# The value products of the preceding step moved in between the turnings of a step's two heads (second block's small attention)

## The chip, the cores and the metric

The kernel runs on one core of a Trainium2 chip. Such a core has TensorE (matrix products, called PE in the rows, its weight loads PEld), VectorE (DVE), ScalarE (ACT), GpSimd (POOL) and SyncE (SP), which work side by side and meet at semaphores. The metric is the time on the device for one execution of the whole program, in microseconds.

## The reference, cut to what matters

Two blocks of two layers each work on 512 tokens of width 1024. In each layer of the second block a mixer stands between two feed-forward networks. One of its parts is an attention with 8 heads of 64 in 2 key groups, in three branches. Two of the branches are computed here as plain causal attentions over all 512 tokens: with 8 blocks of 64 tokens the selection of 8 takes all of them, and the window is 512.

```python
s_s = jnp.einsum('bqgrd,bgqkd->bgrqk', qb, k_sel)
p_s = masked_softmax(s_s, (kpos <= t[:, None])[:, :, None])
o_s = jnp.einsum('bgrqk,bgqkd->bqgrd', p_s.astype(v_sel.dtype), v_sel)
...
s_w = jnp.einsum('bqgrd,bkgd->bgrqk', qb, k_win)
p_w = masked_softmax(s_w, mask_w)
o_w = jnp.einsum('bgrqk,bkgd->bqgrd', p_w.astype(v_win.dtype), v_win)
o = gb[..., 0:1] * o_c + gb[..., 1:2] * o_s + gb[..., 2:3] * o_w
```

## The kernel before, in words

The two branches are one object, `PairedAttention`, with 24 steps in a layer (`steps` = 2 branches x 12). A step handles two heads at once (b = 0 and 1) and one or two query tiles of 128 tokens. Steps come in threes: the first has the tile with four key blocks, the second the tile with three, the third the tiles with two and one. So `blocks(s)` is 4, 3, 3.

What each engine does for a step s:

- `score` (L536), TensorE: queries times keys into a PSUM bank, two steps ahead. It waits until the maxima of the steps up to s - 2 are taken.
- `maximum` (L612), VectorE: mask, scale and row maximum of the scores of both heads.
- `exponentials` (L582), ScalarE: the exponentials of both heads with their row sums.
- `turn` (L546), TensorE: transposes the probabilities of one head, block by block, into the PSUM bank of that head. It waits for that head's exponentials and for the copy of the same head in the step before.
- the copies: VectorE copies head 0 (L621), ScalarE head 1 (L592, behind the exponentials of the next step). The copy of step s - 1 on ScalarE comes after the exponentials of step s.
- `weigh` (L559), TensorE: the value products of a step. They wait for both copies, and in each third step (s % 3 == 0) for the output bank to be taken.
- `take_output` (L2579), ScalarE: copies the finished output of three steps out of its bank. In the second branch it waits for VectorE's addition of the first branch (L2702).

Around the steps `after(s)` places other work. On TensorE: a product of the pooling part (L2447) in steps 3 and 6, and the spread coefficients (`spread_coefficients`, L2434) in steps 15 to 18. On VectorE: the finishing of the gated linear attention in steps 0 to 7 (L2712 to L2714), and the scaling and adding of the first branch (L2698, L2702) in steps 15 to 18. Behind step 23 TensorE spreads the coefficients of the second branch and begins the output projection (L333, L341).

The order on each engine is the order in which the code is written; the engines take their instructions in that order. Between the small attention of a layer and its surroundings the big weights flow through their own ring: SyncE loads them, ScalarE or VectorE rounds, GpSimd subtracts.

Of the kernel before, what the change touches and what calls it, by code (L numbers as in the profile page):

```python
# [144 lines left out]
def build(nc, dr, out):  # L145
    ctx = ExitStack()
    with ctx:
# [112 lines left out]
        class Project:  # L260
# [115 lines left out]
            def after(self, j, act):  # L376

                u = self.jobs[j][0] if j >= 0 else -1
                if j + 1 == len(self.jobs) or self.jobs[j + 1][0] != u:
                    self.stream.round(act, act.copy, RAW, WP, u + 1 + SLOTS)  # L380
# [3 lines left out]
        class Attention:  # L384
# [56 lines left out]
            def tensor(self, pe):  # L441
                for s in range(self.steps):
                    if s + 2 < self.steps:
                        self.score(pe, s + 2)
                    self.turn(pe, s)
                    if s >= 1:
                        self.weigh(pe, s - 1)
                self.weigh(pe, self.steps - 1)
# [47 lines left out]
        class PairedAttention:  # L496
# [67 lines left out]
            def tensor(self, pe, after):  # L564
                for s in range(self.steps):
                    self.turn(pe, s, 0)
                    self.turn(pe, s, 1)
                    if s + 2 < self.steps:
                        self.score(pe, s + 2)
                    if s >= 1:  # L570
                        self.weigh(pe, s - 1)
                    after(s)
                self.weigh(pe, self.steps - 1)

# [2580 lines left out]
```

## Time and profile before

| what | us |
|---|---|
| median of 3 runs | 3177.47 (3176.85 to 3179.08) |
| profiled execution, its own time | 3176.42 |
| span of the profiled execution | 3174.6 |
| TensorE busy | 3070.6 (97%) |
| VectorE busy | 1241.9 (39%) |
| ScalarE busy | 928.7 (29%) |
| GpSimd busy | 1391.7 (44%) |

The span is the time from the first to the last instruction in the trace; the execution's own time is a little longer. The small attention of the first layer lies at about 1616 to 1697 us, that of the second at 2654 to 2735. The shares of the engines over the whole span tell little about them, since the program is mostly large products. In the rows a time at the start is microseconds from the start of the span; the number behind it is a duration. The bracket at the end is the idle time of the engine just before, and what released it; "issue" is time in which it waited for nothing that the profile shows.

### The profile page before, as it was taken

How to read it: one execution, taken by the hardware profiler on the slowest of the kernel's cores; microseconds unless marked ns; L12 is line 12 of the kernel's file. 1: busy time of each engine (PE TensorE's matmuls, PEld its weight loads, DVE VectorE, ACT ScalarE, POOL GpSimd, SP SyncE). 2: the span in 40 equal slices, each digit the busy share in tenths (PEclk: the TensorE clock that was granted, in tenths of full speed). 3: DMA queues.
4: the chain of work that ended last, by engine and by line, in shares of the span. 5: the costliest groups of instructions: out<-in, count | busy, mean ns of one | idle time of the engine just before them, and what ended most of it. 6: DMA issues, size and time to landing. Idle time of an engine off the chain costs nothing. (4 is left out here: it accounts for less than half of the span.)

```text
span 3174.6 us, 39298 instructions
## 1 busy us (share of the span) xinstructions
PE 3070.6 (97%) x15352; PEld 2478.9 (78%) x15352; DVE 1241.9 (39%) x1997; ACT 928.7 (29%) x1623; POOL 1391.7 (44%) x1074
## 2 busy tenths in 40 slices
PE   8999999989999999999999999999999999999998
PEld 5887777778777788887767888878888776788886
DVE  8466244746433222222375322332222237532233
ACT  4356442435453211103463211021110346421101
POOL 2443445524343545445341544454444434154542
PEclk8999999999999999999999999999999999999999
DMA  6222315213231222232110222222222221022222
GB/s 262 100 82 105 101 57 210 103 67 113 87 110 40 73 101 92 85 97 95 67 41 28 93 97 93 91 90 101 98 85 92 86 80 41 28 92 93 88 91 72
DMA packets 45861, 287.78 MB, mean 91 GB/s; under 512 B 5496, under 2 KB 6008, under 8 KB 18680
## 3 DMA queue, kind: packets, MB, share of 16 engines
q1 hardware_dynamic: 42480, 270.32, 24.2%
q10 hardware_dynamic: 3240, 15.53, 1.5%
q8 instruction: 95, 1.56, 0.2%
q14 instruction: 46, 0.38, 0.0%
HBM read 283.67 MB, written 2.16 MB: 90 GB/s over the span
## 5 line engine op out<-in xcount | busy, mean ns | idle before, releaser
L1926 POOL TENSOR_TENSOR w_parts<-w_raw,w_parts 128x512 fp32r<-128x512 f32 (+1 forms) x544 | 703.2, 1321 | 752.9 <-DVE w_parts L2061 702.4
L1986 PE MATMUL PS<-x_parts,w_parts 128*128 128x512 f32 x4224 | 961.1, 390 | 4.5 <-ACT x_parts L799 4.5
L1986 PEld LDWEIGHTS PS<-x_parts,w_parts 128*128 128x128 f32 x4224 | 793.4, 188 | 173.7 <-issue 5.3
L139 POOL TENSOR_TENSOR w_parts<-w_raw,w_parts 128x512 fp32r<-128x512 f32 x380 | 532.6, 1432 | 820.4 <-ACT w_parts L128 790.6
L369 PE MATMUL PS<-x_parts,w_parts 128*128 128x512 f32 x2784 | 698.6, 397 | 14.8 <-POOL w_parts L139 13.7
L369 PEld LDWEIGHTS PS<-x_parts,w_parts 128*128 128x128 f32 x2784 | 521.2, 189 | 135.5 <-POOL w_parts L139 17.8
L2027 PE MATMUL PS<-hidden_parts,w_parts 128*128 128x512 f32 x2112 | 482.9, 390 | 0.0
L2027 PEld LDWEIGHTS PS<-hidden_parts,w_parts 128*128 128x128 f32 x2112 | 396.2, 188 | 83.8 <-issue 1.9
L2068 DVE TENSOR_TENSOR ffn_buffers<-PS,ffn_buffers 128x512 f32<-128x512 f32 x88 | 60.9, 692 | 732.1 <-PE PS L1986 708.9
L128 ACT CAST w_parts<-w_raw 128x2048 fp32r<-128x2048 f32 (+1 forms) x92 | 172.1, 1870 | 140.6 <-PE PS L369 52.3
L2061 DVE CAST w_parts<-w_raw 128x2048 fp32r<-128x2048 f32 (+1 forms) x144 | 156.9, 1089 | 113.4 <-PE PS L2027 113.4
L2045 ACT CAST hidden_parts<-ffn_buffers 128x512 f32 (+1 forms) x88 | 55.0, 625 | 483.8 <-DVE ffn_buffers L2068 483.8
L313 PE MATMUL PS<-w_parts,x_parts 128*128 128x512 f32 x768 | 185.4, 399 | 1.4 <-ACT ssd_buffers L1389 1.4
L313 PEld LDWEIGHTS PS<-w_parts,x_parts 128*128 128x128 f32 x768 | 143.8, 188 | 38.4 <-issue 7.2
L2043 ACT ACTIVATE ffn_buffers<-PS 128x512 f32<-128x512 f32 x88 | 52.7, 599 | 338.3 <-PE PS L1986 338.3
L2087 DVE SCALAR_TENSOR_TENSOR x_all<-PS,x_all 128x512 f32<-128x512 f32 x32 | 22.1, 692 | 225.6 <-PE PS L2027 225.6
L1769 ACT ACTIVATE ffn_buffers<-x_all 128x512 f32<-128x512 f32 x28 | 17.6, 633 | 290.5 <-DVE x_all L2087 231.7
L372 PE MATMUL PS<-w_parts,x_parts 128*128 128x256 f32 x768 | 96.6, 285 | 3.0 <-POOL w_parts L139 3.0
L372 PEld LDWEIGHTS PS<-w_parts,x_parts 128*128 128x128 f32 x768 | 93.3, 192 | 6.7 <-POOL w_parts L139 3.9
L582 ACT ACTIVATE mixer_buffers<-mixer_buffers 128x512 f32<-128x512 f32 (+3 forms) x128 | 70.6, 553 | 25.9 <-DVE mixer_buffers L612 25.9
L369 PE MATMUL PS<-mixed_low,w_parts 128*128 128x512 f32 x192 | 75.9, 396 | 0.0
L333 PE MATMUL PS<-x_parts,w_parts 128*128 128x512 f32 x192 | 54.8, 415 | 10.0 <-ACT x_parts L1874 8.6
(396 smaller groups left out, 3116.2 us busy)
## 6 DMA issues: line engine op xcount, KB each, us to landing
w_raw<-in_w_gu SPq DMA_DIRECT2D x88, 1024.0 KB, 4.7
w_raw<-in_w_in SPq DMA_DIRECT2D x70, 1024.0 KB, 4.8
w_raw<-in_w_d SPq DMA_DIRECT2D x64, 704.0 KB, 4.0
w_raw<-in_w_out SPq DMA_DIRECT2D x24, 1024.0 KB, 4.8
m_all<-in_w_next SPq DMA_DIRECT2D x14, 1024.0 KB, 8.2
m_all<-in_w_gate SPq DMA_DIRECT2D x8, 1024.0 KB, 4.8
ssd_buffers<-decay_rows ACTq DMA_DIRECT2D x16, 512.0 KB, 3.9
m_all<-in_w_next ACTq DMA_DIRECT2D x2, 1024.0 KB, 14.1
```

What stands on the lines that cost most here:

```text
L128: op(parts[:, self.slot(u), 0, 0:n], raw[:, self.slot(u), 0:n]).then_inc(self.high, 1)
L139: last = pool.tensor_tensor(parts[:, self.slot(u), 1, at:to], raw[:, self.slot(u), at:to], parts[:, self.slot(u), 0, at:to].bitcast(F32), ...
L313: last = pe.matmul(PS[:, self.bank(j), 0:m], XS[:, a, kt * second + k, c * P:(c + 1) * P], w[b][:, k, :], start=(not second and k == 0 and ...
L369: last = pe.matmul(PS[0:m, self.bank(j), :], w[a][:, k, c:c + m], part(b, k), start=start, stop=stop)
L372: last = pe.matmul(PS[:, j % 2, 0:m], part(a, k)[:, c * P:(c + 1) * P], w[b][:, k, :], start=start, stop=stop)
L582: act.activation(self.p[:, s % 2, b, at:at + n], self.p[:, s % 2, b, at:at + n], ACT.Exp, bias=self.nm[:, 2 * tile + b:2 * tile + b + 1], ...
L1926: last = pool.tensor_tensor(WP[:, b, 1, at:to], RAW[:, b, at:to], WP[:, b, 0, at:to].bitcast(F32), ALU.subtract)
L1986: return pe.matmul(PS[:, 2 * b + g, :], WP[:, slot(b), w, c:c + P], XS[:, x, k, :], start=start, stop=stop)
L2027: last = pe.matmul(PS[:, 4 + m % 2, :], WP[:, slot(b), w, k * P:(k + 1) * P], hid[:, x, b * KH + k, :], start=(b == k == n == 0), stop=(b ...
L2045: act.copy(flat(hid[:, 0, bass.ds(u, 1), :]), pt[:, b, :]).then_inc(self.hid_high, 1)
L2061: dve.tensor_copy(WP[:, slot(b), 0, 0:n], RAW[:, slot(b), 0:n]).then_inc(self.high, 1)
L2068: dve.tensor_tensor(pt[:, b, :], PS[:, 2 * b + 1, :], gs[:, b, :], ALU.mult).then_inc(self.product, 1)
```

## The change

In `PairedAttention.tensor` the value products of step s - 1 stand between the turning of head 0 and the turning of head 1 of step s. The scores of step s + 2 stand behind both, as before, and are now the last of the step.

```diff
             def tensor(self, pe, after):
                 for s in range(self.steps):
                     self.turn(pe, s, 0)
+                    if s >= 1:
+                        self.weigh(pe, s - 1)
                     self.turn(pe, s, 1)
                     if s + 2 < self.steps:
                         self.score(pe, s + 2)
-                    if s >= 1:
-                        self.weigh(pe, s - 1)
                     after(s)
                 self.weigh(pe, self.steps - 1)
```

The rows below are TensorE's program; `x6` counts instructions as written. L546 are turnings, L536 scores, L559 value products. First two steps of the second branch of the second layer (steps 12 and 13), before the change:

```order
L546 MATMUL PS<-cst,mixer_buffers 128x128 x8
L536 MATMUL PS<-mixer_buffers 128x256 x2
L536 MATMUL PS<-mixer_buffers 128x128 x2
L559 MATMUL PS<-mixer_buffers 64x128 x6
L546 MATMUL PS<-cst,mixer_buffers 128x128 x6
L536 MATMUL PS<-mixer_buffers 128x512 x2
L559 MATMUL PS<-mixer_buffers 64x128 x8
```

The same two steps on TensorE after it:

```order
L546 MATMUL PS<-cst,mixer_buffers 128x128 x4
L559 MATMUL PS<-mixer_buffers 64x128 x6
L546 MATMUL PS<-cst,mixer_buffers 128x128 x4
L536 MATMUL PS<-mixer_buffers 128x256 x2
L536 MATMUL PS<-mixer_buffers 128x128 x2
L546 MATMUL PS<-cst,mixer_buffers 128x128 x3
L559 MATMUL PS<-mixer_buffers 64x128 x8
L546 MATMUL PS<-cst,mixer_buffers 128x128 x3
L536 MATMUL PS<-mixer_buffers 128x512 x2
```

Each run of turnings is cut in two by the value products, and the scores now touch the turnings of the next step.

The second place is steps 15 to 17 on TensorE, where L2434, the spread coefficients, end each step. It begins with those of step 15. Before:

```order
L2434 MATMUL PS<-cst,mixer_buffers 64x128 x8
L546 MATMUL PS<-cst,mixer_buffers 128x128 x6
L536 MATMUL PS<-mixer_buffers 128x512 x2
L559 MATMUL PS<-mixer_buffers 64x128 x8
L2434 MATMUL PS<-cst,mixer_buffers 64x128 x8
```

After:

```order
L2434 MATMUL PS<-cst,mixer_buffers 64x128 x8
L546 MATMUL PS<-cst,mixer_buffers 128x128 x3
L559 MATMUL PS<-mixer_buffers 64x128 x8
L546 MATMUL PS<-cst,mixer_buffers 128x128 x3
L536 MATMUL PS<-mixer_buffers 128x512 x2
L2434 MATMUL PS<-cst,mixer_buffers 64x128 x8
```

The value products of step 15, which wait for an output tile to be taken, had all turnings and the scores of step 16 ahead of them and now have one head's turnings.

The third place is the end of the attention on TensorE, steps 22 and 23 and the coefficients of the second branch. Before:

```order
L546 MATMUL PS<-cst,mixer_buffers 128x128 x6
L559 MATMUL PS<-mixer_buffers 64x128 x8
L546 MATMUL PS<-cst,mixer_buffers 128x128 x6
L559 MATMUL PS<-mixer_buffers 64x128 x12
L2434 MATMUL PS<-cst,mixer_buffers 64x128 x32
```

After:

```order
L546 MATMUL PS<-cst,mixer_buffers 128x128 x3
L559 MATMUL PS<-mixer_buffers 64x128 x8
L546 MATMUL PS<-cst,mixer_buffers 128x128 x6
L559 MATMUL PS<-mixer_buffers 64x128 x6
L546 MATMUL PS<-cst,mixer_buffers 128x128 x3
L559 MATMUL PS<-mixer_buffers 64x128 x6
L2434 MATMUL PS<-cst,mixer_buffers 64x128 x32
```

The last two sets of value products stood together behind the last turning; now the last turning stands between them.

The other engines' instructions and their order are the same.

## Rows read from the trace of the kernel before

**Rows 1.** Timeline, first layer, TensorE: value products of step 15 (start, duration, ...).

```profile
1670.55 1.09 PE L559 MATMUL PS<-mixer_buffers 128*64 128x128 f32 x16 [0.42 <-ACT mixer_buffers L2579]
```

**Rows 2.** Chain of waits, second layer, steps 9 to 12 (start, duration, what).

```profile
2686.57 1.02 PE PS L546 x8
...
2688.44 0.81 PE PS L559 x12
...
2690.05 1.06 PE PS L536 x4
...
2692.94 0.84 PE PS L536 x4
...
2694.59 1.02 PE PS L546 x8
```

**Rows 3.** Windows: TensorE, its loads, VectorE, ScalarE, GpSimd busy; clock, DMA share, GB/s.

```profile
2670.00:2676.00 6.00, 6.00 (x54) 4.11 (x52) 5.86 (x17) 4.51 (x12) 0.00 (x0) 1.00 0.00 0
```

**Rows 4.** Chain of waits, second layer, steps 15 to 18.

```profile
2705.30 0.90 PE PS L2434 x16
...
2707.73 0.59 ACT mixer_buffers L2579
...
2708.46 1.09 PE PS L559 x16
2709.55 0.89 PE PS L2434 x16
...
2714.55 0.63 PE PS L546 x4
```

**Rows 5.** Timeline, second layer: TensorE's weight loads and two of its products.

```profile
2646.23 1.77 PE L536 MATMUL PS<-mixer_buffers 64*128 64x512 f32 x8 [0.69 <-ACT mixed L2489]
2647.93 0.44 PE L2375 MATMUL PS<-cst,mixer_buffers 128*128 128x128 f32 x2
...
2689.18 0.64 PEld L546 LDWEIGHTS PS<-cst,mixer_buffers 128*128 128x128 f32 x6 [0.17 <-issue]
2689.98 0.30 PEld L536 LDWEIGHTS PS<-mixer_buffers 64*128 64x128 f32 x4 [0.17 <-issue]
...
2712.60 0.91 PEld L2434 LDWEIGHTS PS<-cst,mixer_buffers 128*64 128x64 f32 x16
...
2730.12 1.36 PEld L559 LDWEIGHTS PS<-mixer_buffers 128*64 128x64 f32 x24 [0.17 <-issue]
```

**Rows 6.** Timeline, second layer, around a maximum and around a tile's copy.

```profile
2663.06 0.55 DVE L612 CUSTOM_DVE_ANT_0 mixer_buffers<-PS,cst 128x384 f32<-128x384 f32 x1
...
2665.33 0.58 ACT L2579 COPY mixer_buffers<-PS 128x512 f32<-128x512 f32 x1
...
2688.37 0.88 PE L559 MATMUL PS<-mixer_buffers 128*64 128x128 f32 x12
2688.49 0.42 DVE L612 CUSTOM_DVE_ANT_0 mixer_buffers<-PS,cst 128x256 f32<-128x256 f32 x1 [0.61 <-PE PS L536]
```

**Rows 7.** Timeline, second layer, the last steps.

```profile
2729.07 0.46 ACT L592 COPY mixer_buffers<-PS 128x384 f32<-128x384 f32 x1
...
2729.67 0.52 PE L546 MATMUL PS<-cst,mixer_buffers 128*128 128x128 f32 x3 [0.55 <-ACT mixer_buffers L592]
...
2730.22 0.48 ACT L592 COPY mixer_buffers<-PS 128x384 f32<-128x384 f32 x1 [0.70 <-PE PS L546]
...
2731.52 3.69 PE L2434 MATMUL PS<-cst,mixer_buffers 128*64 128x128 f32 x64
```

**Rows 8.** What line 2579 waited for, second layer (us, times).

```profile
  PE PS L559: 4.3, 4
```

**Rows 9.** Timeline and chain around step 8, and the window with its clock.

```profile
2681.57 0.55 PE L546 MATMUL PS<-cst,mixer_buffers 128*128 128x128 f32 x3 [3.24 <-ACT mixer_buffers L582]
...
2683.77 1.58 PE PS L536 x4
...
2684.00:2686.00 2.00, 2.00 (x12) 0.92 (x12) 0.60 (x3) 0.54 (x3) 0.00 (x0) 0.50 0.00 0
```

## The prediction

> Names: in step s of the small attention the TensorE program holds T0 and T1 (the turnings of the two heads, L546), S (the scores of step s+2, L536) and W (the value products of step s-1, L559); in four steps also F (the spread coefficients, L2434). Times are of the second layer; the first layer repeats the pattern to 0.01 us at the places read [rows 1].
>
> **What bounds the kernel now.** I read the chain of waits over the attention first, then the timeline of TensorE's weight loads, then VectorE and ScalarE around single steps. In the second half of each attention the chain never leaves TensorE from step 9 to step 15: three steps take 2694.59 - 2686.57 = 8.02 us, and the pieces fill them without a hole [rows 2]. So there a step costs what TensorE's instructions cost. Steps 1 to 7 are VectorE's: 5.86 of 6 us busy [rows 3], because it also finishes the gated attention's tiles there. From step 15 to 23 the chain hops: F, VectorE's scaling, ScalarE's taking of an output tile (L2579), W, F, and so on [rows 4]. Behind the attention TensorE runs into the output projection without a hole, so what is late at the last F (2731.52) is late at the end. The profiled execution took 3176.42 us (span 3174.6); the median shown is 3177.47, 1.05 above.
>
> **What a change of kind costs.** T uses the array as 128\*128, S as 64\*128, W and F as 128\*64. Between kinds the weight loads show 0.17 us of idle put down to nothing but issue: W to T at 2689.18, T to S at 2689.98, and, at the end of the attention, T to W at 2730.12. Where the kind stays (W to F, 2712.60) no idle is shown [rows 5]. Six turnings take 0.64 us, so three take 0.32. S leaves no such sign in the loads, but S with 512 columns takes 1.06 and with 384 takes 0.84 [rows 2]: the four quarters of difference are 0.22, so 512 columns would be 0.87 and about 0.2 is fixed. From S to a turning the same shows: eight score instructions and the change take 1.70 (2646.23 to 2647.93) [rows 5], 1.49 of it columns at the same rate. The Trainium skill says as much in "TensorEngine Tiling (Array Packing)", Key Properties: changing the tiling mode drains the engine. By that rule the trace agrees, and it speaks against this change.
>
> **The change, part by part.** Nothing is computed anew; W moves from behind S to between T0 and T1. Orders on the other engines and the DMA queue are untouched. Before, a step has three changes of kind (T-S, S-W, W-T), now four (T0-W, W-T1, T1-S, S-T0). In steps with F: before three (W-F costs none), now five.
>
> (a) TensorE-bound steps, 9 to 15: six steps x 0.17 = 1.02, and step 15, with F, 0.17 + 0.2 = 0.37. Together 1.39. Step 8 adds nothing: its extra change lies in the wait for ScalarE's copy, which W inherits from T1.
>
> Does W now wait in these steps? It needs the copy of head 1 that T1 needed at the same place, so no wait is added by that. But S now comes just ahead of the next step, so the loop S, maximum, exponentials, copy, W has lost W's cover. The tightest is the one with an output tile in it: 0.12 from the end of S to VectorE (2688.37 to 2688.49), 2.27 from the maximum to the tile's copy (2663.06 to 2665.33) [rows 6], and 0.73 from there to W [rows 4] = 3.12. TensorE has in that time one whole step, a third of 8.02 and one change, 2.84, and T0 of three turnings with its change, 0.49: 3.33. It fits by 0.2, so 0 is added; if it missed, VectorE and ScalarE would set the pace at a few tenths a step.
>
> (b) Step 16. Its W needs the tile taken (L2579), and that needs VectorE's addition behind F of step 15 [rows 4]. Before, T1 and S stood ahead of W and were done in this wait, with 0.42 still left. Now they stand behind: from W to the F of step 16 TensorE must do, besides W, the change 0.17, T1 0.32 + 0.17 and S 1.06 = 1.72. That F is on the chain (2709.55, then VectorE's scaling and maximum, ScalarE's exponentials and copy, TensorE again at 2714.55), so 1.72 late. What is queued behind the waiting W is T1, S and F; VectorE waits for all three.
>
> (c) Steps 17 and 18: TensorE reaches W of step 18 about 0.15 behind the copy, and one change more stands ahead of F: 0.3 together. Steps 19 to 22: W and T1 wait for the same copies, order inside does not count; the exponentials of step 23 started behind W and an output tile (1.08 us waited) and now start behind S: + 0.15.
>
> (d) The end. Before, T1 of step 23 started at 2729.67, then W of 22, and under it ScalarE's copy (2730.22); W of 23 followed with no wait, F at 2731.52: 1.85. Now: W of 22 0.64, change 0.17, T1 start to copy 0.55, copy to TensorE 0.60 (2729.07 to 2729.67), W of 23 0.64 = 2.60 [rows 5, 7]. The copy has lost its cover: + 0.75 to 0.8.
>
> (e) Steps 1 to 7: S ends later by W of the step and a change, at most 1.02 + 0.17 (W of four blocks: 16 loads at the rate of 2730.12, and its change). VectorE's own load covers it: it goes into its maximum at 2663.06 with no idle before it [rows 6] and is full in the whole window [rows 3]. Cost 0; with that cover gone it would be 0.17 a step, 1.2 a layer.
>
> Sum per layer 1.39 + 1.72 + 0.3 + 0.15 + 0.8 = 4.36; two layers 8.7. 3176.42 + 8.7 = 3185.1 on the profiled execution's scale, 3186.2 on the median's. I take 3186.
>
> Bounds. T0-W was read once, at a place where both sides were ready; if the four-change order paid nothing for it, (a) would be 0 and (b) to (d) about 2.2 per layer: 3181.9. Below nothing only by the first rival. Above: the clock, the third rival.
>
> **Rivals.**
> Faster: W earlier lets ScalarE take the output tile earlier. It waited for W four times in a layer, 4.3 us [rows 8]. If these waits carry the pace, up to 1.08 at each of those that lie on the chain would come back. Against it: three of the four lie in the TensorE-bound steps, and the fourth is replaced by S's wait. Giving the full 1.08 at the last one in both layers, with free changes and (d) hidden, and (b) halved, it is 2 x (0.86 - 1.08) = -0.4; to be faster by more than 0.2% (6.4 us, about what a measurement of this kernel can tell) all three mid ones must count too: 3177.5 + 2 x 0.86 - 8.6 = 3170.6. It decides from where ScalarE, not TensorE, ends last before W.
>
> No measurable change: the changes of kind are free, (b) and (d) alone remain: 3181.9, + 0.14%. For it: 0.17 is put down to "issue", not to a named cause. Against: it appears at each change of kind in either direction.
>
> More slower: the clock. Before step 8 TensorE idled 3.24 us, and then ran at 0.50 of full speed, the lower of the levels 1.2 and 2.4 GHz; S with 384 columns took 1.58 there [rows 9] against 0.84, and T1, S and W together, 2.14 at full speed, by the same ratio 4.0. In step 16 the idle time ahead of W grows from 0.42 to about 2. If the clock falls there too, up to 1.9 per layer more, of which I take 1.5: 3189. The Trainium skill, "TensorE: Matmul & The Clock Gate", on practice, warns only of idle gaps over some 3 us; by that rule it does not happen. For falling: the time around is full of small matmuls; against: the idle time stays shorter than the one that was followed by a fall.
>
> **Numbers.** Forecast as summed 0.62; clock rival 0.12; free changes 0.21; faster rival 0.05. Of the forecast's cases a tenth or so ends under +0.2% (3183.8) by terms that are smaller than read. So slower 0.68, same 0.28, faster 0.04. The range that holds 8 in 10 reaches to the free-changes case below and to the clock case above: 3181 to 3189.5.
>
> **What would show it.** In the trace after: three steps of 9 to 14 take 8.5 us instead of 8.02, the weight loads with 0.17 of idle on both sides of W; in step 16 W still waits for the tile's copy, now about 2 us, and F starts 2.8 instead of 1.1 us behind W's start; at the end W of 23 waits for ScalarE's copy; VectorE's steps 1 to 7 unmoved; granted clock 1.00 around step 16. It would be wrong if T0 to W shows no idle, if W in steps 10 and 13 waits for ScalarE (more), or if the last F moves less than 4 us against the attention's start.

## The result, and the profile after

| runs | before | after | ratio (95%) |
|---|---|---|---|
| first set | 3178.96 (3176.85 to 3179.73, 7 runs) | 3187.91 (3186.31 to 3191.68, 7 runs) | 1.0033 [1.0023, 1.0043] |
| the same kernel once more | 3177.12 | 3188.69 (3187.55 to 3190.46, 5 runs) | 1.0037 [1.0023, 1.0050] |
| profiled execution | 3176.42 | 3189.43 | |

The change makes the kernel slower, by 0.33% in the first set. The median of before shown ahead of the prediction, 3177.47, was that of its first three runs. The medians of the 7 runs differ by 8.95 us and those of the second set by 11.57 (ratios of 1.0033 and 1.0037, some 10.5 and 11.8 us); the forecast was 8.7. The traces tell more than these medians. I measure an attention from the first turning of step 0 to the first coefficient product behind step 23:

| us | before | after | difference |
|---|---|---|---|
| first layer | 1616.29 to 1693.61 = 77.32 | 1617.48 to 1700.52 = 83.04 | +5.72 |
| second layer | 2654.01 to 2731.52 = 77.51 | 2661.38 to 2744.57 = 83.19 | +5.68 |

So 11.4 of the 13.0 us between the profiled executions lie in the two attentions; 1.2 arose ahead of the first one and 0.4 between and behind them. Per layer that is 1.3 more than the 4.36 of the sum. The page's totals:

```profile
span 3187.6 us, 39298 instructions
...
PE 3078.3 (97%) x15352; PEld 2479.8 (78%) x15352; DVE 1242.0 (39%) x1997; ACT 930.8 (29%) x1623; POOL 1393.0 (44%) x1074
```

VectorE, ScalarE and GpSimd are busy as long as before to 2 us. TensorE shows 7.7 us more, though its work is the same: its instructions are longer somewhere.

**Steps 9 to 14.** The chain of waits of the second layer, from T0 of step 12 to T0 of step 15, answers to [rows 2]:

```profile
2702.46 0.59 PE PS L546 x4
2703.05 0.81 PE PS L559 x12
2703.85 0.59 PE PS L546 x4
2704.44 0.85 PE PS L536 x8
...
2710.94 0.59 PE PS L546 x4
```

Still all TensorE, and a step now has four pieces instead of three. Three steps (12, 13, 14) take 2710.94 - 2702.46 = 8.48, where it was 8.02: 0.46, or 0.153 a step. The weight loads of the second layer, here of step 10, show where, as [rows 5] did:

```profile
2697.22 0.85 PEld L559 LDWEIGHTS PS<-mixer_buffers 128*64 128x64 f32 x16 [0.17 <-issue]
2698.24 0.31 PEld L546 LDWEIGHTS PS<-cst,mixer_buffers 128*128 128x128 f32 x3 [0.17 <-issue]
2698.72 0.30 PEld L536 LDWEIGHTS PS<-mixer_buffers 64*128 64x128 f32 x4 [0.17 <-issue]
```

The idle 0.17 stands on both sides of the value products now. A border between two groups costs little where the kind stays: the six turnings of [rows 5] are those of both heads, each with a wait of its own, and take 0.64 without a hole.

**Step 16**, first layer, TensorE:

```profile
1669.59 1.09 PE L2434 MATMUL PS<-cst,mixer_buffers 128*64 128x128 f32 x16
1670.62 0.55 PE L546 MATMUL PS<-cst,mixer_buffers 128*128 128x128 f32 x3
1672.97 1.47 PE L559 MATMUL PS<-mixer_buffers 128*64 128x128 f32 x16 [1.80 <-ACT mixer_buffers L2579]
1674.37 0.90 PE L546 MATMUL PS<-cst,mixer_buffers 128*128 128x128 f32 x3
1675.20 1.98 PE L536 MATMUL PS<-mixer_buffers 64*128 64x512 f32 x4
1677.11 1.09 PE L2434 MATMUL PS<-cst,mixer_buffers 128*64 128x128 f32 x16
```

The wait of W is 1.80 instead of 0.42 [rows 1], since T1 and S no longer stand in it. From W to F it is 1677.11 - 1672.97 = 4.14; before it was 0.89 (1670.55 to 1671.44; the chain in [rows 4] sets F of this step 0.2 later than the timeline does). But not only are there more instructions: each is longer. T1 takes 0.90, two rows above 0.55. The windows (columns as in [rows 3]) say why:

```profile
1672.00:1674.00 2.00, 1.03 (x15) 1.06 (x16) 1.73 (x10) 1.76 (x6) 0.00 (x0) 0.88 0.00 0
1674.00:1677.00 3.00, 3.00 (x12) 1.04 (x8) 0.00 (x0) 1.06 (x5) 0.00 (x0) 0.51 0.00 0
1677.00:1680.00 3.00, 3.00 (x38) 2.21 (x36) 1.72 (x3) 0.00 (x0) 0.00 (x0) 1.00 0.00 0
```

After the idle 1.80 us the granted clock stood at 0.51 for three microseconds, the lower of its two levels (1.2 and 2.4 GHz). Meanwhile VectorE shows 0.00: it waits for F. The second layer has the same wait of 1.80 and the same fall:

```profile
2719.00:2721.00 2.00, 2.00 (x7) 0.50 (x6) 0.00 (x0) 0.48 (x1) 0.00 (x0) 0.50 0.00 0
```

There W starts at 2717.08 and F at 2720.97, 3.89 later, and F itself takes 1.30 instead of 1.09: the stretch at the lower clock begins a little later and reaches into F.

**The end**, chain of waits of the second layer, against [rows 7]:

```profile
2741.88 0.88 PE PS L559 x12
2742.76 0.49 PE PS L546 x3
2743.25 0.02 issue
2743.28 0.49 ACT mixer_buffers L592
2743.76 0.14 issue
2743.90 0.88 PE PS L559 x12
```

ScalarE's copy is on the chain now: the value products of step 23 wait for it.

**ScalarE's waits.** What line 2579 waited for in the second layer, against [rows 8]:

```profile
  PE PS L559: 1.1, 1
```

Three of four waits, 3.2 us, are gone. Nothing ended earlier by that.

### The profile page after: what moved, and what is told of

It is laid out like the page before. It is cut to its first block and busy times, and to the rows that moved or that the text cites. A ratio compares the mean times of both kernels' runs of the same rounds, so it can differ in the third digit from the quotient of the medians.

```text
span 3187.6 us, 39298 instructions
## 1 busy us (share of the span) xinstructions
PE 3078.3 (97%) x15352; PEld 2479.8 (78%) x15352; DVE 1242.0 (39%) x1997; ACT 930.8 (29%) x1623; POOL 1393.0 (44%) x1074
## 5 line engine op out<-in xcount | busy, mean ns | idle before, releaser
L1986 PE MATMUL PS<-x_parts,w_parts 128*128 128x512 f32 x4224 | 961.7, 390 | 4.5 <-ACT x_parts L799 4.5
L369 PE MATMUL PS<-x_parts,w_parts 128*128 128x512 f32 x2784 | 696.7, 396 | 15.4 <-POOL w_parts L139 14.3
L612 DVE CUSTOM_DVE_ANT_0 mixer_buffers<-PS,cst 128x512 f32<-128x512 f32 (+3 forms) x128 | 56.1, 487 | 27.9 <-PE PS L536 27.7
```

The lines of the kernel that those rows point to most:

```text
L369: last = pe.matmul(PS[0:m, self.bank(j), :], w[a][:, k, c:c + m], part(b, k), start=start, stop=stop)
L612: dve.tensor_tensor_reduce(self.p[:, s % 2, b, at:at + n], PS[:, 2 * (s % 2) + b, at:at + n], const("causal")[:, T - n:T], -(HD ** -0.5), ...
L1986: return pe.matmul(PS[:, 2 * b + g, :], WP[:, slot(b), w, c:c + P], XS[:, x, k, :], start=start, stop=stop)
```

## The experiments

Pieces and attentions are read from the profiled executions; a time given with a ratio, or for the whole program, is the median of the runs. W in step 16 means, as in the prediction, the value products that stand in step 16 of TensorE's program (those of step 15). In the diffs "-" is the kernel before, where nothing else is said. Kernels with added lines have the line numbers behind them shifted by 2 to 5 in their rows.

### Step 16 and the clock

The changed kernel once more:

> The changed kernel unaltered, profiled and timed again. Theory (changes of kind, lost cover in step 16 and at the end, and a fall of the granted clock behind the longer idle time of step 16): each small attention takes 5.7 us more than before from its first turning to the spread coefficients of the second branch (83.0 against 77.3), of which about 1.5 is the clock in step 16 (granted clock about 0.5 there). Rival (the clock fell by chance of that one execution): the three instruction groups behind the wait of step 16 run at full speed in one or both layers, value products to spread coefficients 2.6 instead of 4.1, and the attention takes 4.2 more.

Attentions 82.96 and 83.23. From W to F of step 16 4.14 and 4.03 us, with 1.80 idle ahead: the clock fell again in both layers.

The new order in step 16 alone:

```diff
+                    between = s == 16
                     self.turn(pe, s, 0)
+                    if s >= 1 and between:
+                        self.weigh(pe, s - 1)
                     self.turn(pe, s, 1)
                     if s + 2 < self.steps:
                         self.score(pe, s + 2)
-                    if s >= 1:
+                    if s >= 1 and not between:
                         self.weigh(pe, s - 1)
```

> The order of the change in step 16 alone, all other steps as before. Theory (lost cover of one turning and the scores behind the wait for the output tile, plus the clock): from the value products of step 15 to the spread coefficients behind them 4.1 us instead of 0.9 in each layer, 3.2 more, at a granted clock near 0.5; the whole attention 3.2 to 3.3 more per layer, the program 6.5 more. Rival (the clock does not fall, since fewer changes of kind came before): 1.7 per layer, 3.5 in all. Rival (the cost of the change lies in the changes of kind): under 0.5 per layer. Steps 9 to 15 as before: three steps 8.02.

3180.95 us, ratio 1.0013 [1.0004, 1.0023]; attentions 80.67 and 80.75, so +3.35 and +3.24. First layer:

```profile
1670.61 1.09 PE L559 MATMUL PS<-mixer_buffers 128*64 128x128 f32 x16 [1.80 <-ACT mixer_buffers L2582]
...
1672.11 1.98 PE L536 MATMUL PS<-mixer_buffers 64*128 64x512 f32 x4
1674.02 1.88 PE L2437 MATMUL PS<-cst,mixer_buffers 128*64 128x128 f32 x16
```

Second layer:

```profile
2713.38 1.09 PE L559 MATMUL PS<-mixer_buffers 128*64 128x128 f32 x16 [1.80 <-ACT mixer_buffers L2582]
...
2714.88 1.13 PE L536 MATMUL PS<-mixer_buffers 64*128 64x512 f32 x4
2715.94 1.09 PE L2437 MATMUL PS<-cst,mixer_buffers 128*64 128x128 f32 x16
```

The same wait of 1.80; in the first layer the scores take 1.98 and F 1.88, in the second 1.13 and 1.09. So the fall doesn't always come. (In the first layer it came late: W still takes 1.09, W to F is 3.41 instead of the expected 4.1, and F carries the rest.) Where it stays away, W to F takes 2.56, which is 1.67 over 0.89: term (b), forecast at 1.72. The second layer lost its other 1.5 elsewhere, in its windows around step 8:

```profile
2686.00:2688.00 2.00, 1.68 (x7) 1.01 (x7) 0.13 (x1) 1.96 (x6) 0.80 (x1) 0.50 0.00 0
2688.00:2690.00 2.00, 2.00 (x16) 1.15 (x12) 1.04 (x4) 0.57 (x2) 0.00 (x0) 0.50 0.00 0
2690.00:2692.00 2.00, 2.00 (x12) 1.57 (x8) 0.66 (x1) 0.74 (x4) 0.00 (x0) 0.50 0.00 0
```

There the clock stayed down for over 6 us (the slow stretch, from here on); the kernel before shows some 3.5 us at this place, where it too idles 3.05 and 3.24 us ahead of step 8 [rows 9]. From T0 of step 8 to W in step 16 it is 2713.38 - 2684.98 = 28.40 here and 2708.46 - 2681.57 = 26.89 before, 1.51 less. So this attention's +3.24 matches the expected 3.2 by luck: 1.67 of it is step 16.

The changed kernel with the wait filled by products that nobody reads (the kernel's own `keep_busy`, in a free bank), first three of them:

```diff
                     self.turn(pe, s, 0)
+                    if s == 16:
+                        pe.wait_ge(self.copied[1], s)
+                        keep_busy(pe, 5, 3)
                     if s >= 1:
                         self.weigh(pe, s - 1)
```

(The unmarked lines are those of the changed kernel.)

> The changed kernel with three products of the identity with a constant (128x512, into the PSUM bank that the next turning overwrites) put into TensorE's wait of step 16, behind the first head's turning. They compute nothing that is used and fill about 1.3 of the 1.8 us of idle time. Theory (the clock fell because of that idle time): the granted clock stays at 1.00, value products to spread coefficients 2.6 instead of 4.1, the attention 81.5 instead of 83.0 per layer, the program 3 less than the changed kernel. Rival (the clock falls for the small matmuls around, whatever stands in the wait): 4.1 as in the changed kernel.

The three took 2.67, more than the wait, so W went 0.7 late: this part of the expectation's price was mis-sized. Attentions 82.14 and 83.52; 3189.15 us, ratio 1.0039 [1.0023, 1.0054]. But W to F was 2.56 and 2.57, at a granted clock of 1.00. The second attention has the longer slow stretch at step 8 again. The same with two products (`keep_busy(pe, 5, 2)`):

> The changed kernel with two unused products (128x512, into the bank that the next turning overwrites) in TensorE's wait of step 16; a product of this kind took 0.87 us in the kernel with three, so two take 1.74 of the 1.80 us of idle time and the value products start on time. Theory: the clock stays at 1.00, value products to spread coefficients 2.6, wait not longer than before, and the attention 81.5 against 83.0 in both layers. Rival (the products only move the loss): 82 or more.

```profile
1670.64 1.88 PE L649 MATMUL PS<-cst 128*128 128x512 f32 x4
1672.60 1.09 PE L559 MATMUL PS<-mixer_buffers 128*64 128x128 f32 x16
...
1675.17 1.09 PE L2437 MATMUL PS<-cst,mixer_buffers 128*64 128x128 f32 x16
```

The window of the same layer:

```profile
1672.00:1675.00 3.00, 2.92 (x25) 1.49 (x23) 1.36 (x9) 2.69 (x10) 0.00 (x0) 1.00 0.03 5
```

No idle, clock 1.00, W to F 1675.17 - 1672.60 = 2.57 in place of 4.14: the clock cost 1.57 us. The first attention is 81.44, 1.6 less than in the changed kernel. The second, 83.03, gained only 0.2: from T0 of step 0 to F of step 15 it took longer, 53.7 against 52.1 in the first layer, again by a longer slow stretch at step 8. One run of the whole: 3186.47.

Taken together, 1.80 us of idle time was followed by the lower clock in 5 of 6 attentions (twice two of the changed kernel, one of two here), and no filled wait was, in 4 of 4. The waits ahead of step 8 say the same. In the twelve kernels profiled here that leave it unfilled it is 2.20 to 3.33 us long, and the lower clock followed in all 24 attentions; in the two that fill it (below) it followed in none of 4. That the idle time causes the fall is shown by this; what decides whether it comes behind 1.80 us is not.

### The other terms

The change everywhere but in step 16, and then everywhere but in 16 and 23 (the diff of before with other conditions, `between = s != 16` and `between = s not in (16, 23)`):

> The order of the change in all steps but 16. Theory: the 1.7 and the clock's 1.5 of step 16 are gone, the changes of kind (1.2) and the end (0.8) stay: the attention 2.3 to 2.6 us more than before per layer (79.8), idle time ahead of the value products of step 16 again 0.4, granted clock 1.00 there; the program 5 more than before. Rival (the loss is spread over the steps, the wait of step 16 only moves to the next tile): the attention stays above 82.

> The order of the change in all steps but 16 and 23. Theory: against the order changed in all steps but 16 (2.4 more than before per layer) the lost cover of the last copy goes too, 0.84: the attention 1.5 to 1.7 more than before (79.0), value products of step 22 to spread coefficients 1.85 again, what stays are the changes of kind. Rival (the end is hidden by ScalarE's tile): 79.8 as without it.

Without 16: 3182.34, ratio 1.0016 [1.0006, 1.0025]; attentions 79.75 and 79.98, +2.43 and +2.47. The sum less (b) is 4.36 - 1.72 = 2.64. Step 16 keeps its short wait and full speed:

```profile
1672.38 1.09 PE L559 MATMUL PS<-mixer_buffers 128*64 128x128 f32 x16 [0.41 <-ACT mixer_buffers L2582]
1673.28 1.07 PE L2437 MATMUL PS<-cst,mixer_buffers 128*64 128x128 f32 x16
```

Without 16 and 23: 3179.84, ratio 1.0010 [1.0001, 1.0020]; attentions 78.91 and 80.26. The first is 0.84 less than without 16 alone: term (d), forecast at 0.8. From the wait for the copy to F it is 1.85 again (1693.24 to 1695.09). In the second layer a longer slow stretch at step 8 hides it: T0 of step 0 to F of step 15 took 53.45, against 52.11 in the first.

### Where the scores stand

Scores between the turnings, value products last. That has four changes of kind too, but no wait of W moved up:

```diff
                     self.turn(pe, s, 0)
-                    self.turn(pe, s, 1)
                     if s + 2 < self.steps:
                         self.score(pe, s + 2)
+                    self.turn(pe, s, 1)
                     if s >= 1:
                         self.weigh(pe, s - 1)
```

> The scores of step s+2 between the two turnings, the value products behind both: first head, scores, second head, value products. As many changes of kind in a step as in the changed kernel (four), but the value products keep their cover. Theory (each change of kind costs 0.17 where TensorE sets the pace, whichever work stands between the turnings): three steps of 9 to 14 take 8.5 us as in the changed kernel, not 8.02; no further loss in step 16 and at the end, and the scores now fill waits between the two turnings in steps 8, 18 and 20, up to 1.3 together: the attention 77.2 to 78.2 against 77.3 before. Rival (the cost of those steps comes from the value products standing early, not from changes of kind): three steps 8.02.

3176.39 against 3176.34, ratio 0.9999 [0.9989, 1.0008]; attentions 77.00 and 77.25, so 0.3 less than before. Its first layer:

```profile
1658.12 0.66 PE L546 MATMUL PS<-cst,mixer_buffers 128*128 128x128 f32 x4
1658.70 0.92 PE L536 MATMUL PS<-mixer_buffers 64*128 64x256 f32 x8
1659.56 0.66 PE L546 MATMUL PS<-cst,mixer_buffers 128*128 128x128 f32 x4
...
1666.60 0.66 PE L546 MATMUL PS<-cst,mixer_buffers 128*128 128x128 f32 x4
```

Three steps (12 to 14) take 1666.60 - 1658.12 = 8.48, exactly as in the changed kernel: with quite other neighbours, the fourth change costs the same 0.15. It is paid back elsewhere. T0 of step 8 to T0 of step 9 takes 3.55 (1645.51 to 1649.06) instead of 5.02 (1643.57 to 1648.59), because the scores of step 10 cover the wait for ScalarE's copy; from there to F of step 15 it is 1.64 more, of which some 0.6 is the slow stretch, which here reaches past T0 of step 9 (its first turnings take 1.12 instead of 0.66) and would otherwise stand in the 3.55, so that without the clock, by an estimate, some 0.9 is gained and 1.05 lost; from F of step 15 to that of 16 4.22 in both; and 0.49 less behind. -1.47 + 1.64 - 0.49 = -0.32. So a change of kind can be worth its price where it fills a wait.

Scores ahead of both turnings in every step (`score(s + 2)` moved to the top of the loop):

> The scores of step s+2 first in each step, then both turnings, then the value products: three changes of kind in a step as before, and the scores ahead of TensorE's waits for the exponentials. Theory (the loss is a matter of what stands behind a waiting instruction; the reverse must gain): three steps of 9 to 14 stay at 8.02; in steps 8 and 20 the scores run inside TensorE's waits of 3.2 and 0.8, which takes 1.5 to 3.5 off each attention (74 to 76 against 77.3), the program 3 to 7 less than before. Rival (the scores' own wait for VectorE's maxima, or the bank that they free later, becomes the bound): the attention at 77 or more.

3176.56 against 3176.34, ratio 0.9999 [0.9990, 1.0008]: the expected 1.5 to 3.5 us per attention did not come. In the first layer, from the last product ahead of the attention (L2382) to the last F it took 79.19 (1615.44 to 1694.63) against 79.11. Behind step 15 it gained: F of step 15 to the last F 25.14 against 26.39. It lost 0.95 at the start, where the scores of step 2 stand ahead of the first turning, and 0.33 from T0 of step 8 to F of step 15, where the clock stayed low longer:

```profile
1647.00:1653.00 6.00, 6.00 (x35) 4.61 (x36) 1.92 (x6) 3.06 (x10) 0.34 (x1) 0.51 0.00 0
```

So the next two kernels keep the order of before in the first steps and put the scores first from step 16, and from step 8:

```diff
+                    if s >= 16 and s + 2 < self.steps:
+                        self.score(pe, s + 2)
                     self.turn(pe, s, 0)
                     self.turn(pe, s, 1)
-                    if s + 2 < self.steps:
+                    if s < 16 and s + 2 < self.steps:
                         self.score(pe, s + 2)
```

> The order of before up to step 15; from step 16 on the scores of step s+2 stand first in the step. Theory: steps 0 to 15 as before (first turning to first spread coefficients 50.9), and from there to the last spread coefficients 25.1 as in the kernel with the scores first everywhere, against 26.4 before: 1.2 less per layer, 2.5 in all, 0.08%, at the edge of what the timing shows. Rival (the gain came from the later start of everything there): 26.4.

> As the kernel with the scores first from step 16, but from step 8. Theory: VectorE's steps 0 to 7 are not touched, so the 1.0 us that the scores-first order lost there is gone. In step 8 the scores run in the wait of 3.2 us, 0.85 us less behind it, but TensorE ran at half speed for 6 instead of 3.7 us behind that wait with the scores first, which took the gain back: from the first turning of step 8 to the first spread coefficients 23.5 to 24.0 against 23.65 before; the attention 75.8 to 76.3. Rival (the long slow spell was chance): 22.8 and 75.2.

From 16: attentions 76.07 and 76.31, 1.25 and 1.20 less; 3175.19 against 3177.65, ratio 0.9995 [0.9986, 1.0004], too little for the timing to tell. From 8: 75.23 and 76.64 (one run, 3174.69). Its two layers differ by 1.4, of which 1.15 is the length of the slow stretch once more: T0 of step 8 to F of step 15 took 22.79 in the first, as the rival had it, and 23.94 in the second, as the theory had it.

### Filling the wait ahead of step 8

With the scores first from step 8, two unread products behind them in step 8:

```diff
+                    if s >= 8 and s + 2 < self.steps:
+                        self.score(pe, s + 2)
+                    if s == 8:
+                        pe.wait_ge(self.copied[0], s)
+                        keep_busy(pe, 4, 2)
                     self.turn(pe, s, 0)
```

(The score below the turnings stands under `s < 8`.)

> As the one before, with two unused products (128x512, into the bank that the next turning overwrites) in the wait of step 8, behind the scores. Theory (the clock falls because TensorE idles in this wait): scores 0.85 and products 1.74 fill 2.6 of 3.2 us, the granted clock stays at 1.00 behind it, and step 8 to the first spread coefficients takes 21.3 us against 23.65 (scores 0.85 and clock 1.5 saved); the attention 73.7 against 77.3, the program 7 us less, 0.2%. Rival (two products are too little, or the second wait of 0.8 us brings the clock down all the same): 23 or more and 75.5.

```profile
1638.36 0.92 PE L536 MATMUL PS<-mixer_buffers 64*128 64x384 f32 x4
1639.20 1.98 PE L651 MATMUL PS<-cst 128*128 128x512 f32 x4
1641.46 0.55 PE L546 MATMUL PS<-cst,mixer_buffers 128*128 128x128 f32 x3 [0.28 <-ACT mixer_buffers L587]
```

The windows behind it:

```profile
1641.00:1645.00 4.00, 2.94 (x28) 2.04 (x28) 1.60 (x5) 4.00 (x16) 2.30 (x2) 1.00 0.00 0
1645.00:1650.00 5.00, 5.00 (x48) 3.48 (x50) 3.42 (x13) 4.36 (x15) 0.00 (x0) 1.00 0.00 0
```

The same part of the program without the filling, where T0 of step 8 starts at 1645.41:

```profile
1645.00:1650.00 5.00, 3.81 (x24) 2.77 (x26) 1.60 (x5) 4.58 (x16) 2.22 (x2) 0.69 0.00 0
```

The idle time ahead of T0 of step 8 is 0.28 instead of 2.20, the clock stays at 1.00, T0 of step 8 to F of step 15 takes 21.23 and 21.22: short, and equal in both layers. Attentions 73.66 and 73.92. The whole: 3170.91 (3167.11 to 3172.56, 11 runs) against 3177.65, ratio 0.9978 [0.9969, 0.9987]. It is faster than both the kernel before and the changed one, though by 0.22% only. Its profiled execution (3167.11) was the fastest of the 11.

The order of before with three unread products ahead of T0 of step 8 (same wait, `keep_busy(pe, 4, 3)`) and nothing else:

> The order of before in all steps, with three unused products (128x512, into the bank that the next turning overwrites, 0.87 us each) in TensorE's wait of step 8, 2.6 of its 3.0 to 3.2 us. Theory (a fall of the clock follows a wait in which TensorE idles, and costs about 1.5 us in each attention of the kernel before too): granted clock 1.00 behind step 8, from its first turning to the first spread coefficients 22.1 instead of 23.65, the attention 75.8 instead of 77.3 to 77.5, the program 3 less (0.1%). Rival (the gain of the kernel with the scores first from step 8 and two products came from the order alone): 23.6 and 77.3, no change.

Attentions 75.74 and 76.00, 1.6 and 1.5 less than before; T0 of step 8 to F of step 15 22.06 in both layers, against 23.65 and 23.56. The clock behind the filled wait, first layer:

```profile
1651.00:1656.00 5.00, 3.95 (x31) 2.41 (x30) 1.92 (x6) 4.63 (x17) 2.39 (x2) 1.00 0.00 0
```

3175.31 against 3177.16, ratio 0.9994 [0.9985, 1.0003]: the gain of 3.1 in the traces is within what the timing leaves open, and its median moved by 1.85. Its profiled execution, 3182.09, was the slowest of its 11: it reached the first attention at 1624.27, 8 us later than the kernel before, which no run here explains. So this kernel shows what the clock costs in the attentions, not that the program gains.

## Why the prediction was right, and what it missed

The first layer, piece by piece, against the terms:

| piece (first layer) | before | after | more | forecast |
|---|---|---|---|---|
| (e) T0 of step 0 to T0 of step 9 | 32.30 | 32.32 | 0.02 | 0 |
| (a) T0 of step 9 to F of step 15 | 18.63 | 19.79 | 1.16 | 1.39 |
| F of step 15 to W in step 16 | 3.33 | 3.38 | 0.05 | 0 |
| (b) W to F in step 16 | 0.89 | 4.14 | 3.25 | 1.72 |
| (c) F of step 16 to T0 of step 21 | 14.67 | 14.93 | 0.26 | 0.3 |
| (c) T0 of step 21 to W in step 23 | 5.65 | 5.79 | 0.14 | 0.15 |
| (d) W in step 23 to F | 1.85 | 2.69 | 0.84 | 0.8 |
| sum | 77.32 | 83.04 | 5.72 | 4.36 |

In the last two rows the mark for before is T1 of step 23 (1691.76), the instruction that waited for the copy where W does now.

- (a) was right in kind and 0.23 high. The fourth change costs 0.153 a step, not 0.17: three steps 8.48 against 8.02. And step 15 costs 0.25 (T0 to F 2.83 instead of 2.58), not 0.37: by an estimate two changes at 0.153 less 0.06, since F behind W was not quite free before (0.70 from W of three blocks to F, against 0.64 for its loads alone). In the first layer, not moving step 16 (+2.43) and moving only it (+3.35) add up to the whole, 5.78 against 5.72.
- (a), further: W never waited for ScalarE in these steps; no row of theirs has idle time ahead of it. The loop kept its pace, as the estimated 0.2 of slack had it; that slack was not measured.
- (b) is the step where it missed. "If the clock falls there too" was given 0.12, and the main case had the "granted clock 1.00 around step 16". By its instructions the term was right: 1.67 and 1.68 with the clock up (the new order in step 16 alone, second layer, and the filled kernels). The clock put 1.57 on top in the first layer (in the second 1.32 up to F and 0.2 in it), where the rival had taken 1.5. That size was partly luck: its 2.14 at full speed for T1, S and W fits the pieces of step 8 (0.49, 0.84 and 0.81); those of step 16 take 2.56. A reading of before was off too: F of step 16 started 0.89 behind W by the timeline, not 1.1, and so 4.14 stand against the 2.8 that the prediction named. The argument against it, that the wait stays shorter than the idle 3.24 us that was followed by a fall, did not hold: 1.80 us was enough in 5 of 6. The Trainium skill, "TensorE: Matmul & The Clock Gate", section "HAM oscillation — how this bites in real kernels", warns of idle gaps over some 3 us; here the clock fell after 1.80 us, and the measurement decides. The prediction had let the page warn "only" of such gaps, which holds for that section and not for the whole page.
- (c), (d) and (e) came out within 0.05. In the second layer (c) is 0.2 more, the part of F at the lower clock. For (d) there is an experiment: with step 23 left as it was, 0.84 came back in the first layer.
- Faster rival: its waits went, 3.2 of 4.3 us, and nothing came of it, for the reason given: TensorE ends last at these places. No change: refuted by the 0.17 on both sides of W and by the 8.48 of two kernels. Changing the tiling mode drains the engine, as the Trainium skill says in "TensorEngine Tiling (Array Packing)", Key Properties; the trace agrees, with 0.153 us for an added change in a step.

So the terms of the sum held, but the case that was given 0.62, with the granted clock at 1.00 around step 16, is not the one that came: beside the terms came the fall of the clock, which was given 0.12. By the traces the right sum is about 4.15 of work and 1.55 of clock in each layer, 11.4 in all, not 8.7. The sum was 2.7 us short, and 3187.91 lies in the stated range because that was drawn up to the clock case. That the forecast of 3186 is only 1.9 off is partly luck: the medians scatter by more than the missing term, and can't tell the two sums apart; they differ by 8.95 and 11.57, and the intervals of the two ratios, 7.3 to 13.7 and 7.3 to 15.9 us, hold both 8.7 and 11.4. The pieces of the traces can. I can't say which of the runs without a trace had the clock down.

Left open: why the clock did not fall in the second layer with the new order in step 16 alone. It is the only one of the six attentions with the wait of 1.80 us in which the slow stretch at step 8 had been the longer one; a single case, which doesn't show a cause. Also open is what sets the length of that stretch (some 3.5 us in 17 of the 24 attentions with the wait ahead of step 8 unfilled, about twice that in 7), and why an execution reaches the first attention up to some us earlier or later with the same work ahead of it.

## What to carry to other kernels

Count the changes of shape in TensorE's stream as instructions with a price, and put what waits longest last: a wait moved ahead of ready work makes that work late in full. Where the idle time ahead of a burst of small products grows to near two microseconds, look at the granted clock behind it, not at the wait alone. (Here 1.80 us was followed by a fall in 5 of 6, while the 1.41 us ahead of the product L2382, just before each attention, was so in none of 28; nothing in between was tried.) Filling such a wait with a few unread products, slightly fewer than fit, took 1.5 to 1.6 us off an attention, as much as the best of the reorderings tried here (0.9 to 2.1). Judge edits of one or two microseconds by pieces of the trace between fixed instructions, and check in each that no stretch at the lower clock, whose length varies, lies between the marks.

## What the hardware showed that I had not expected

- The kernel before itself paid for the clock: filling the idle time ahead of step 8 took 1.5 to 1.6 us off each attention with not one useful instruction moved.
- The slow stretch behind a like idle time is not always of one length. From T0 of step 8 to F of step 15, one kernel (scores first from step 8) took 22.79 in one layer and 23.94 in the other; filled, 21.23 and 21.22.
- After 1.80 us of idle time the clock fell or did not, with the same instructions around it: scores with 512 columns took 1.98 or 1.13. After 2.20 us and more it fell in all 24 cases.
- The fourth change of kind costs 0.153 us a step whether it is made by the value products or by the scores: both orders need 8.48 for three steps.
